# Laying the high and low parts of each squared-unit block next to each other in SBUF

## What is computed

```
h = layer_norm(ALPHA * x + y, ln1_g[i], ln1_b[i])
r = jax.nn.relu(h @ mlp_w1[i])
f = (r * r) @ mlp_w2[i]
e = (p[i] @ ple_w[i]) * jax.nn.sigmoid(h @ ple_gate_w[i])
x = layer_norm(ALPHA * h + f + e, ln2_g[i], ln2_b[i])
```

## Time and profile before

| | |
|---|---|
| time, median of 3 runs | 2128.34 us (2124.19 to 2129.76) |
| profiled execution | 2127.4 us |
| its span, first to last instruction | 2125.6 us |
| PE busy | 2115.1 us, 13221 matmuls |
| DVE busy | 1267.7 us (60%) |
| ACT busy | 822.9 us (39%) |
| mean share of the DMA engines busy | 26% |
| granted TensorE clock | 0.999 |

### The profile page before, as it was taken

How to read it: one execution, slowest core, us unless ns; L and a number is a source line. 1 busy time by engine, 2 the same in 40 slices (tenths; PEclk the granted TensorE clock), 3 DMA queues, 4 the chain that set the end, 5 groups by cost and what they waited for, 6 DMA issues and landing times.

```text
span 2125.6 us, 31857 instructions
## 1 busy us (share of the span) xinstructions
PE 2115.1 (100%) x13221; PEld 2112.9 (99%) x13221; DVE 1267.7 (60%) x1892; ACT 822.9 (39%) x1288; POOL 74.3 (3%) x67
## 2 busy tenths in 40 slices
PE   9999999999999999999999999999999999999998
PEld 9999999999999999999999999999999999999998
DVE  5232357786454443444777777888875455545477
ACT  3221233653433322222543544555444324333345
POOL 0000000000000000000020002000300000000000
PEclk9999999999999999999999999999999999999999
DMA  4010231444223111111112244443222211122133
GB/s 174 30 59 30 69 129 47 129 132 134 67 80 99 50 40 50 40 60 41 60 41 99 88 138 139 154 140 120 72 77 90 70 50 61 59 80 80 62 107 132
DMA packets 53778, 179.68 MB, mean 85 GB/s; under 512 B 8081, under 2 KB 10513, under 8 KB 53649
## 3 DMA queue, kind: packets, MB, share of 16 engines
q1 hardware_dynamic: 50768, 177.33, 25.6%
q10 hardware_dynamic: 2880, 0.52, 0.1%
HBM read 173.36 MB, written 4.46 MB: 84 GB/s over the span
## 4 chain that ended last, share of the span: by engine, by line
PE 98%; ACT 1%; DVE 1%; issue 0%; DVEq 0%; POOL 0%; ACTq 0%; POOLq 0%
PE ps L697 32%; PE ps L699 32%; PE ps L698 32%; ACT acc L955 0%; PE ps L862 0%; PE ps L726 0%; PE ps L722 0%; PE ps L732 0%; DVE acc L1173 0%; PE ps L750 0%; PE ps L749 0%; DVE std L1213 0%; ACT w_split L880 0%; PE ps L781 0%; DVE acc L1297 0%
## 5 line engine op out<-in xcount | busy, mean ns | idle before, releaser
L697 PE MATMUL ps<-h_hi,w_split 128*128 128x352 f32 x2160 | 697.5, 323 | 1.4 <-ACT t L1005 0.6
L699 PE MATMUL ps<-h_hi,w_split 128*128 128x352 f32 x2160 | 696.0, 322 | 0.0
L698 PE MATMUL ps<-h_lo,w_split 128*128 128x352 f32 x2160 | 694.1, 321 | 0.0
L697 PE MATMUL ps<-r_hi,w_split 128*128 128x352 f32 x1634 | 527.0, 323 | 0.1
L699 PE MATMUL ps<-r_hi,w_split 128*128 128x352 f32 x1634 | 526.4, 322 | 0.0
L698 PE MATMUL ps<-r_lo,w_split 128*128 128x352 f32 x1634 | 524.9, 321 | 0.0
L1297 DVE TENSOR_TENSOR acc<-acc,ps 128x352 f32<-128x352 f32 (+1 forms) x769 | 375.2, 518 | 135.4 <-PE ps L699 134.7
L616 DVE TENSOR_TENSOR w_split<-w_raw,w_split 128x1024 fp32r<-128x1024 f32 x291 | 357.8, 1251 | 111.9 <-ACT w_split L880 111.2
L697 PEld LDWEIGHTS ps<-h_hi,w_split 128*128 128x128 f32 x2160 | 405.7, 188 | 2.7 <-issue 1.5
L699 PEld LDWEIGHTS ps<-h_hi,w_split 128*128 128x128 f32 x2160 | 408.0, 189 | 0.0
L698 PEld LDWEIGHTS ps<-h_lo,w_split 128*128 128x128 f32 x2160 | 406.6, 188 | 0.0
(11 more groups left out here) (128 smaller groups left out, 1196.1 us busy)
## 6 DMA issues: line engine op xcount, KB each, us to landing
w_raw<-w_stream SPq DMA_DIRECT2D x315, 512.0 KB, 3.5
x_raw<-x_t SPq DMA_DIRECT2D x4, 704.0 KB, 8.1
y_t<-acc SPq DMA_DIRECT2D x4, 704.0 KB, 4.2
w_raw<-p_t SPq DMA_DIRECT2D x6, 352.0 KB, 2.9
y_t<-acc SPq DMA_DIRECT2D x3, 352.0 KB, 2.2
w_raw<-w_stream SPq DMA_DIRECT2D x3, 256.0 KB, 4.8
x_raw<-x_t SPq DMA_DIRECT2D x4, 176.0 KB, 4.0
x_raw<-x_t SPq DMA_DIRECT2D x2, 352.0 KB, 5.7
```

The source lines that it names most:

```text
L697: pe.matmul(out, wh, mov_h, start=first, stop=False)
L698: pe.matmul(out, wh, mov_l, start=False, stop=False)
L699: return pe.matmul(out, wl, mov_h, start=False, stop=last)
```

## The change

One tensor of the same total size takes the place of `r_hi` and `r_lo`: six blocks, each with its 352 high columns and then its 352 low columns. `rh` and `rl` become views of it. The three-matmul pattern, the order of all steps, all semaphores, and what lies before and behind the region stay as they are. A block's low part now begins 1408 bytes behind its high part, and two high blocks of one part are 2816 bytes apart, so the two instructions that split token inputs write two runs of 352 elements with a gap between them, where they wrote one run of 704.

```diff
-        rh, at = place("r_hi", [P, NG * CHUNK * TG], F32R, at3)
-        rl, at = place("r_lo", [P, NG * CHUNK * TG], F32R, at)
+        r_both, at = place("r", [P, NG * CHUNK, 2, TG], F32R, at3)
+        rh, rl = r_both[:, :, 0, :], r_both[:, :, 1, :]
         tt, at = place("t", [P, 2, TG], F32, at)
...
         def rpart(t, n, f):
-            at = (n * CHUNK + f) * TG
-            return t[:, at:at + TG]
+            return t[:, n * CHUNK + f, :]
+
+        def rparts(t, n):
+
+            return t[:, n * CHUNK:(n + 1) * CHUNK, :]
+
+        def token_inputs(u):
+            return raw[:, u.q, 0:KP * TG].rearrange("p (k t) -> p k t", k=KP)
...
             if isinstance(slot, tuple):
-                cols = slice(slot[1] * KP * TG, (slot[1] + 1) * KP * TG)
-                ins = eng.tensor_tensor(rl[:, cols], raw[:, u.q, 0:KP * TG], f32(rh[:, cols]), ALU.subtract)
+                ins = eng.tensor_tensor(rparts(rl, slot[1]), token_inputs(u), f32(rparts(rh, slot[1])), ALU.subtract)
...
                 if isinstance(slot, tuple):
-                    n = slot[1]
-                    act.copy(rh[:, n * KP * TG:(n + 1) * KP * TG], raw[:, u.q, 0:KP * TG]).then_inc(w_hi, 1)
+                    act.copy(rparts(rh, slot[1]), token_inputs(u)).then_inc(w_hi, 1)
```

## The result

The changed kernel takes 2135.04 us (median of 7 runs, 2133.86 to 2137.59) against 2127.66 (7 runs, 2124.19 to 2129.76): ratio 1.0036, 95% interval 1.0026 to 1.0045. It is slower by 7.4 us, just beyond the 0.3% that I took as telling a change from none, and outside my range of 2123 to 2133.

A forecast was written before the change was run, and what follows sets the result against it. PE was taken as the bound, its matmul count times pitch. Terms summed 0 + 0 + 0 + 0, leaving the profiled 2127.4 us; forecast 2128 us, range 2123 to 2133, chance of same 0.92.

The forecast's parts named there:

- What bounds the kernel: Whole span: PE, busy 2115.1 of 2125.6 us, sets the time by matmul count times pitch; its waits total 2.6 us.
- What PE reads: The 4890 matmuls on r: only addresses differ, so pitch stays; 0, bounds -5.4 to +8.8 us.
- the bounds that I had from the pitches: Matmuls on r: pitches between 158.8 and 160.6 ns seen across four stretches, giving -5.4 to +8.8 us.
- my trial of a distance in the trace: PE passing from h (33792 bytes apart) to r (8448) at 909.87: 160 ns each, so distance does not matter.
- pitch up: Matmuls on r: adjacent high and low blocks, or neighbours being written, slow PE's reads; +8.8 us at full size, chance 0.07.
- The sign that I named: Profile after: forecast is wrong if r's matmul pitch parts from h's in the same stretch by over 1 ns.
- Neighbours written while PE reads: ACT and DVE writing blocks next to those PE reads: no effect, 0 us, within the same pitch bounds.
- The Trainium skill's: Rule that engines contend only at the VectorE and GpSimd port pair; makes the written-neighbours term exactly 0.
- The six splits: Token-input splits on ACT and DVE: two runs of 352 cost 0 more, upper bound +1.17 us each.
- the 192 writes: Writes at L1017 and L1283 on each engine: still one block of 352 contiguous columns, cost 0.
- code: Instruction loading: no instruction more or less, so nothing more to load; 0.
- The range: Whole kernel: 2123 to 2133 us, from the spread of runs before plus a smaller part of the pitch bounds.

The follow-up runs named there:

- pairs near: Kernel before, with r as one tensor, each part's two high blocks then its two low blocks, high and low 2816 bytes apart; ratio 0.9996.
- far, shifted: Kernel before, with one ReLU buffer placed between the high and low regions, so high and low are 9856 bytes apart; ratio 1.0056.
- changed, 128 lower: Changed kernel with the whole tensor 128 bytes lower; ratio 1.0010 to the kernel before.
- PE alone: PE repeats the steps on constant data in four placements, other engines still; run again with weights 128 bytes further; changed placement's up steps then 3866 to 3873 ns.
- padded, at 0: Changed layout with blocks padded to 1536 bytes, all starting at a multiple of 256; ratio 1.0008 to the kernel before.
- padded, at 128: Changed layout with blocks padded to 1536 bytes, all starting 128 past a multiple of 256; ratio 1.0012 to the kernel before.

## Why the prediction was wrong

**What bounds the kernel** held: PE, by count times pitch, with 3 us of waits. That the pitch was the only way to a change of any size, and that it differed between stretches for a reason no view gave, was read rightly. I then left that sign unexplained.

**What PE reads: I took 0, and this is the step that failed.** The runs put 7.4 us there, inside the bounds that I had from the pitches (-5.4 and +8.8). Two errors led to the 0. First, I took the region's start and the set of block addresses as all that could matter and dismissed their order; but the change turns the sequence 128/128, 0/0 into 128/0, 128/0. Second, my trial of a distance in the trace was none: 33792 and 8448 bytes are both multiples of 256, so high and low start at the same place modulo 256 in h and in r. A distance of 1408 bytes, 5.5 times 256, was outside what the trace had tried. The equal mean lengths (323 against 323), which I took as further evidence, say nothing of the pitch: L702 on `h_hi` still has 323 in the changed kernel, whose up steps are 30 ns longer.

**The rival "pitch up"** (+8.8 us, to which I gave 0.07) came near in size by luck. Its mechanism, reads of r made slower by a near neighbour or by one that is being written, is refuted: "pairs near" is near and loses nothing, "far, shifted" is far and loses no less, and "changed, 128 lower" has the very neighbours of the changed kernel and loses 0.1%. Nor are the added nanoseconds on the 4890 matmuls of r that its price was worked out from.

**The sign that I named** (the pitch of r parts from that of h in the same stretch by over 1 ns) came: in layer 0 a mean h step of 3870 ns is 161.2 ns a matmul, a mean r step of 3838 ns is 159.9. But it points at the wrong tensor if it is read as I meant it. The r steps kept 3834 to 3840 ns, and the h steps beside them went from 3840 to 3870, though h did not move. My reading is that the places of one step's operands set the pattern in which PE begins the next; no run shows how.

**Neighbours written while PE reads: 0** was right. PE alone shows the lengths of the changed and the shifted kernel with nobody writing. **The Trainium skill's** rule ("SBUF — State Buffer", "Who interferes with whom") that PE waits on no other engine agrees with that, and I let it stand for more than it says: it is about other engines, and this is PE and its own reads.

**The six splits: 0** was right (781 and 892 ns against 782 and 892), as was 0 for the 192 writes and for code.

**The range** was cut to 2133 "for the smaller part" of the pitch bounds, without a reason from rows. With the bounds at full size it would have held the result.

## What to carry to other kernels

Where PE is busy all the time with matmuls like these (352 float32r columns, a weight load each), the start of each operand modulo 256 bytes is worth trying out: blocks of 352 float32 columns (5.5 times 256 bytes) alternate between two places, and moving two tensors by 128 bytes was worth 0.4% here. Before a change that only reorders blocks in SBUF is called free, write down the places modulo 256 in the order in which PE reads them. No rule was found that gives the time from the places, so each has to be run. And when a pitch differs between stretches with the clock the same, take the lengths of whole steps from the timeline before calling it unknown: here the values repeated to 1 or 2 ns, which meant a pattern and not noise.

## What the runs showed of the hardware

A stream of 352-column float32r matmuls, each with its own weight load, has a pitch that depends on addresses, with PE working alone. In the streams at the end of those two runs, triples on a start at a and on a start at b (both modulo 256) take turns; mean pitch in ns:

| a, b | weights at 0 | weights at 128 |
|---|---|---|
| 0, 0 | 160.00 | 158.32 |
| 128, 128 | 166.67 | 160.00 |
| 0, 128 | 161.10 | 159.99 |
| 64, 64 | 159.99 | 159.98 |
| 0, 64 | 161.11 | 160.00 |

The windows that bear on the largest of these, weights at 0, streams 0, 0 and 128, 128:

```profile
1510.00:1550.00 40.00, 40.00 (x252) 1.00 0.00 1
1557.00:1597.00 40.00, 40.00 (x242) 1.00 0.00 1
```

Of the two real kernels with one place for all r blocks (weights at 128), "padded, at 0" fits in most of its down steps: 158.32 x 24 = 3800 ns. But it has 4000 ns = 24 x 166.67 as a second length, which these streams show only for weights at 0, and "padded, at 128" takes mostly 3867 ns = 24 x 161.1 for its down steps where its stream gives 160.00 x 24 = 3840. So the table doesn't forecast a kernel. The same sequence of addresses can have more than one length (3813, 3840, 3867), held for up to hundreds of microseconds and mostly changed where PE stands still or does two matmuls more; which one a stretch takes differs from execution to execution. That this is most of the 5 us over which runs of one kernel spread is likely, but was not shown. The changed and the shifted placement, with weights at 128, held one set of lengths in every round. What in PE makes these patterns was not found; no run tried other widths or other types.
